# RWKV-7 scan of an encoder layer: heads stacked on partitions, an inverse and its transpose kept in PSUM, three chunks in one TensorE order

## The reference

```python
def step(S, inp):                       # S: (B, H, 64, 64), f32
    r_t, w_t, k_t, v_t, kk_t, a_t = inp
    sa = jnp.einsum('bhij,bhj->bhi', S, -kk_t)
    S = (S * w_t[:, :, None, :] + sa[..., None] * (kk_t * a_t)[:, :, None, :]
         + v_t[..., None] * k_t[:, :, None, :])
    y = jnp.einsum('bhij,bhj->bhi', S, r_t)
    return S, y
_, y = lax.scan(step, zeros, xs, reverse=reverse)   # y of both directions is added
```

## Time and profile before

| What | Value |
|---|---|
| median of 2 runs | 4515.17 us (4513.25 to 4517.09) |
| profiled execution, its own time | 4511.47 us |
| span of its trace | 4509.7 us |
| mean granted TensorE clock | 0.944 of full |
| instructions | 73891 |
| TensorE busy | 86% of the span, 30776 matmuls |
| DVE / ScalarE / GpSimd busy | 49% / 24% / 11% |
| mean DMA rate | 54 GB/s |

### The profile page before, as it was taken

One profiled execution on the slowest core, in us unless ns is written; L12 is line 12 of the kernel. 1 busy time (PEld: TensorE's weight loads), 2 busy tenths in 40 slices (PEclk: granted clock), 3 DMA queues, 4 the chain that ended last, 5 costly groups with the idle time before them and its releaser, 6 DMA issues. The chain is left out here.

```text
span 4509.7 us, 73891 instructions
## 1 busy us (share of the span) xinstructions
PE 3898.8 (86%) x30776; PEld 3260.3 (72%) x30776; DVE 2232.0 (49%) x2980; ACT 1070.0 (24%) x1635; POOL 500.4 (11%) x407
## 2 busy tenths in 40 slices
PE   7999999988997355588888886888788899999997
PEld 6888888866885342477777764676677788888886
DVE  4445444462002757777777754242224444444445
ACT  2111111122112455333333333222222111111112
POOL 0000000010000420243344321010001000000000
PEclk9999999998998677899999997998899999999999
DMA  2111011002222026311111122300110101101101
GB/s 100 41 42 39 30 42 42 19 10 108 84 84 114 1 84 190 112 52 35 52 52 52 35 83 70 121 14 29 38 33 19 52 28 42 42 30 40 42 19 47
DMA packets 70916, 244.32 MB, mean 54 GB/s; under 512 B 5056, under 2 KB 30912, under 8 KB 64320
## 3 DMA queue, kind: packets, MB, share of 16 engines
q1 hardware_dynamic: 64528, 219.56, 14.2%
q10 hardware_dynamic: 6192, 21.89, 1.2%
HBM read 185.38 MB, written 56.05 MB: 54 GB/s over the span
## 5 line engine op out<-in xcount | busy, mean ns | idle before, releaser
L292 DVE TENSOR_TENSOR main_acc<-main_acc,ffn_psum 128x512 f32<-128x512 f32 (+1 forms) x1056 | 617.3, 598 | 855.1 <-PE ffn_psum L215 854.4
L204 PE MATMUL ffn_psum<-x_xh,ffn_wi_h 128*128 128x512 f32 (+1 forms) x2112 | 525.0, 357 | 52.5 <-DVE ffn_wi_l L281 52.5
L204 PE MATMUL ffn_psum<-x_xl,ffn_wi_h 128*128 128x512 f32 (+1 forms) x2112 | 525.2, 357 | 0.0
L204 PE MATMUL ffn_psum<-x_xh,ffn_wi_l 128*128 128x512 f32 (+1 forms) x2112 | 525.2, 357 | 0.0
L204 PEld LDWEIGHTS ffn_psum<-x_xh,ffn_wi_h 128*128 128x128 f32 x2112 | 372.5, 188 | 120.2 <-DVE ffn_wi_l L281 52.9
L204 PEld LDWEIGHTS ffn_psum<-x_xh,ffn_wi_l 128*128 128x128 f32 x2112 | 350.1, 189 | 60.3
L204 PEld LDWEIGHTS ffn_psum<-x_xl,ffn_wi_h 128*128 128x128 f32 x2112 | 349.6, 188 | 60.9
L215 PE MATMUL ffn_psum<-ffn_hid_h,ffn_wo_h 128*128 128x512 f32 (+1 forms) x1056 | 381.3, 361 | 12.9 <-DVE ffn_hid_l L300 10.0
L215 PE MATMUL ffn_psum<-ffn_hid_h,ffn_wo_l 128*128 128x512 f32 (+1 forms) x1056 | 378.1, 358 | 0.0
L215 PE MATMUL ffn_psum<-ffn_hid_l,ffn_wo_h 128*128 128x512 f32 (+1 forms) x1056 | 377.4, 357 | 0.0
L256 ACT CAST ffn_hid_h<-ffn_hid 128x1280 fp32r<-128x1280 f32 x44 | 55.7, 1265 | 1090.4 <-DVE ffn_hid L298 1090.4
(11 more groups left out here) (315 smaller groups left out, 6756.3 us busy)
## 6 DMA issues: line engine op xcount, KB each, us to landing
ffn_w_raw_in<-ffn_w_in_dram SPq DMA_DIRECT2D x44, 1024.0 KB, 6.8
rws_pack<-pack SPq DMA_DIRECT2D x40, 900.0 KB, 4.6
ffn_w_raw_out<-ffn_w_out_dram SPq DMA_DIRECT2D x44, 512.0 KB, 3.6
proj<-mixin_stage ACTq DMA_DIRECT2D x27, 640.0 KB, 3.0
mixin_w_raw<-mix_w_in_dram SPq DMA_DIRECT2D x27, 512.0 KB, 3.5
pack<-rwp_pack SPq DMA_DIRECT2D x4, 2580.0 KB, 10.7
rwp_raw<-proj SPq DMA_DIRECT2D x15, 640.0 KB, 8.5
kv_w_raw<-ca_w_kv_dram SPq DMA_DIRECT2D x16, 512.0 KB, 3.5
```

Of the source, the lines that this page charges most:

```text
L204: mm = nc.tensor.matmul(ps[:, at + c * BANK:at + c * BANK + tn], w[:, slot, cols], x[:, k, t0:t0 + tn], start=(k == 0 and j == 0), stop=(k ...
L292: nc.vector.tensor_tensor(acc[:, o, t0:t0 + tn], acc[:, o, t0:t0 + tn], ps[:, at:at + tn], ALU.add).then_inc(added, 1)
```

## The change

The phase is written anew for the same mathematics. Head 0 of each pair stays on lanes 0 to 63 and head 1 on lanes 64 to 127 throughout, with no padding: every tile is 128 x (2 directions x 4 pairs x 64), and one product works on 64 lanes of one half of the array (`own`) or crosses from one half's lanes to the other half's outputs (`other`). The whole-array transposes go. Where the transpose of X was needed, a second matrix Z, the transpose, is built beside X: both stay in PSUM over all levels, and a level adds to them by accumulating products (`extend`); ScalarE copies each of them out after every level. Transposed rows of b and k are made by products with a 64x64 identity (`turn_rows`); v is transposed once, in the preparation, and loaded by its own DMA. Each instruction of DVE, ScalarE and GpSimd covers both directions where it covered one. The decay edge of a chunk is folded into one factor (`carry`), so h takes one product a chunk. GpSimd makes the scaled b, k, a and r and the first level; DVE keeps the masks, h and the addition to the output. In a step n three chunks are in work: the state of n, levels 1 to 5 of the inverse of m = n + 1, and the products of p = n + 2; the step list runs from n = -2. Buffers hold two to four chunks. In the masks, `before_pair` and `upto` give way to `within` and `first` of the same widths.

All that concerns a group of products has this form; `state_u`, `state_out`, `with_rows`, `turn_rows` and `first_x` are built like those shown, with 16, 48, 32 (128 columns wide), 32 and 16 products.

```diff
-R_COL, V_COL, G_COL = 0, C, 2 * C
+V_COL, R_COL, G_COL = 0, C, 2 * C
...
+        V_GROUPS = tuple((g, min(8, N_CHUNKS - g), (6 + n % 2) * BANK) for n, g in enumerate(range(0, N_CHUNKS, 8)))
...
+                pe.wait_ge(next_added, 6 * (t + 2))
+                for n, (c0, cn, at) in enumerate(V_GROUPS):
+                    if n == 2 or t:
+                        pe.wait_ge(v_set, 3 * t + max(n - 1, 0))
+                    for c in range(cn):
+                        for h in range(2):
+                            lanes = slice(h * C, (h + 1) * C)
+                            mm = nc.tensor.matmul(ps[lanes, at + c * C:at + (c + 1) * C], vr[lanes, (c0 + c) * C:(c0 + c + 1) * C],
+                                                  stack_ident[lanes], start=True, stop=True)
+                    mm.then_inc(v_turned, 1)
...
-                nc.scalar.copy(part(V_COL), view(vr[:])).then_inc(copied, 1)
+                for n, (c0, cn, at) in enumerate(V_GROUPS):
+                    act.wait_ge(v_turned, 3 * t + n + 1)
+                    nc.scalar.copy(pack[:, c0:c0 + cn, V_COL:V_COL + C], ps[:, at:at + cn * C].rearrange("p (c t) -> p c t", t=C)).then_inc(v_set, 1)
...
+        BOTH, PAIR, EDGED = [P, 2, 4, C], [P, 2, 4, 2, C], [P, 2, 4, C + 1]
+        pack, v = slots("pack", [P, 2, 4, PACK - R_COL], 2), slots("v", BOTH, 4)
+        x, z, y, inverse = m_.sb("x", BOTH), m_.sb("z", BOTH), m_.sb("y", BOTH), m_.sb("inverse", BOTH)
+        AT_X, AT_Z, AT_Y, AT_U, AT_H, AT_O = range(6)
+        AT_GB, AT_GK, AT_ROWS = (6, 7), (5, 6), (7, 4)
...
+            for c in range(N_CHUNKS):
+                if c >= 2:
+                    sp.wait_ge(exps, 2 * (c - 1))
+                    sp.wait_ge(bk_set, 2 * (c - 1))
+                    sp.wait_ge(ar_set, 2 * (c - 1))
+                if c >= 4:
+                    sp.wait_ge(o_done, c - 3)
                 for d in DIRS:
+                    sp.dma_start(pack[c % 2][:, d], pack_d[chunk_of(c)[d]][:, :, R_COL:PACK]).then_inc(loaded[c % 2], 16)
+                    sp.dma_start(v[c % 4][:, d], pack_d[chunk_of(c)[d]][:, :, V_COL:V_COL + C]).then_inc(loaded[c % 2], 16)
...
+            def scale(c):
+                pool.wait_ge(loaded[c % 2], 64 * (c // 2 + 1))
+                pool.wait_ge(exps, 2 * (c + 1))
+                if c >= 2:
+                    pool.wait_ge(b_turned, c - 1)
+                    pool.wait_ge(k_turned, c - 1)
+                nc.gpsimd.tensor_tensor(bk[c % 2][:, :, :, 0], packed(c, B_COL), now(grown[c % 2]), ALU.mult).then_inc(bk_set, 1)
+                nc.gpsimd.tensor_tensor(bk[c % 2][:, :, :, 1], packed(c, K_COL), now(grown[c % 2]), ALU.mult).then_inc(bk_set, 1)
+                if c >= 3:
+                    pool.wait_ge(o_done, c - 2)
+                nc.gpsimd.tensor_tensor(ar[c % 3][:, :, :, 0], packed(c, KK_COL), before(decayed), ALU.mult).then_inc(ar_set, 1)
+                nc.gpsimd.tensor_tensor(ar[c % 3][:, :, :, 1], packed(c, R_COL), now(decayed), ALU.mult).then_inc(ar_set, 1)
+                if c >= 1:
+                    if c >= 4:
+                        pool.wait_ge(h_set, c - 2)
+                    nc.gpsimd.tensor_tensor(carry[(c - 1) % 3][:], edge(grown[(c - 1) % 2]), edge(grown[c % 2]), ALU.mult).then_inc(carried, 1)
+            def first_level(c):
+                pool.wait_ge(masked_b, 2 * (c + 1))
+                nc.gpsimd.tensor_tensor(first[:], gb[c % 2][:, :, :, 0], first_mask, ALU.mult).then_inc(first_set, 1)
+                pool.wait_ge(first_set, c + 1)
+                if c:
+                    pool.wait_ge(z_done, ZS * (c - 1) + 1)
+                nc.gpsimd.tensor_tensor(w0[:], first[:], all_ident, ALU.add).then_inc(w0_set, 1)
+            def step(n, m, p):
+                if p is not None:
+                    scale(p)
+                    first_level(p)
...
+            def first_z(c):
+                pe.wait_ge(w0_set, c + 1)
+                if c:
+                    pe.wait_ge(inverse_set, c)
+                for n, (d, q) in enumerate(TILES):
+                    for e in range(2):
+                        mm = product(bank(AT_Z)[other(e), col(d, q)], stack_ident[own(e)], w0[own(e), d, q], start=(n == 0), stop=False)
+                mm.then_inc(z_done, 1)
+            def lower(c, level):
+                pe.wait_ge(x_set, XS * c + level)
+                if level > 1 or c:
+                    pe.wait_ge(y_set, XS * c + level - 1)
+                for d, q in TILES:
+                    for e in range(2):
+                        mm = product(bank(AT_Y)[other(e), col(d, q)], gb[c % 2][own(e), d, q, 0], x[own(e), d, q])
+                mm.then_inc(y_done, 1)
+            def extend(c, level):
+                pe.wait_ge(y_set, XS * c + level)
+                pe.wait_ge(z_set, XS * c + level)
+                for d, q in TILES:
+                    if level < LEVELS - 1:
+                        for e in range(2):
+                            mx = product(bank(AT_X)[own(e), col(d, q)], z[other(e), d, q], y[other(e), d, q], start=False)
+                    for e in range(2):
+                        mz = product(bank(AT_Z)[other(e), col(d, q)], y[other(e), d, q], z[other(e), d, q], start=False)
+                if level < LEVELS - 1:
+                    mx.then_inc(x_done, 1)
+                mz.then_inc(z_done, 1)
+            def state_rhs(n):
+                pe.wait_ge(h_set, n + 1)
+                pe.wait_ge(masked_k, 2 * (n + 1))
+                if n:
+                    pe.wait_ge(u_set, n)
+                o = bank(AT_U)
+                for d, q in TILES:
+                    for e in range(2):
+                        product(o[other(e), col(d, q)], gk[n % 2][own(e), d, q, 0], v[n % 4][own(e), d, q], stop=False)
+                    for e in range(2):
+                        mm = product(o[other(e), col(d, q)], ar[n % 3][own(e), d, q, 0], h[n % 2][own(e), d, q], start=False)
+                mm.then_inc(rhs_done, 1)
...
+            def state_h(n):
+                pe.wait_ge(u_set, n + 1)
+                pe.wait_ge(b_rows_set, n + 1)
+                pe.wait_ge(k_rows_set, min(n + 2, N_CHUNKS))
+                o = bank(AT_H)
+                for d, q in TILES:
+                    for e in range(2):
+                        product(o[own(e), col(d, q)], k_rows[n % 2][own(e), d, q], v[n % 4][own(e), d, q], stop=False)
+                    for e in range(2):
+                        mm = product(o[own(e), col(d, q)], b_rows[n % 2][own(e), d, q], u[own(e), d, q], start=False)
+                mm.then_inc(h_done, 1)
...
+            def step(n, m, p):
+                if n >= 0:
+                    state_rhs(n)
+                if m is not None:
+                    first_z(m)
+                    lower(m, 1)
+                if n >= 0:
+                    state_u(n)
+                if m is not None:
+                    extend(m, 1)
+                if n >= 0:
+                    state_h(n)
+                if m is not None:
+                    lower(m, 2)
+                if n >= 0:
+                    state_out(n)
+                if m is not None:
+                    extend(m, 2)
+                if p is not None:
+                    with_rows(p, 0, AT_GB, with_b)
+                if m is not None:
+                    lower(m, 3)
+                if p is not None:
+                    with_rows(p, 1, AT_GK, with_k)
+                if m is not None:
+                    extend(m, 3)
+                if p is not None:
+                    turn_rows(p, 0)
+                if m is not None:
+                    lower(m, 4)
+                if p is not None:
+                    turn_rows(p, 1)
+                if m is not None:
+                    extend(m, 4)
+                    lower(m, 5)
+                if p is not None:
+                    first_x(p)
+                if m is not None:
+                    extend(m, 5)
...
+            def take_x(c, level):
+                act.wait_ge(x_done, XS * c + level + 1)
+                if level or c:
+                    act.wait_ge(y_done, XS * c + level)
+                nc.scalar.copy(x[:], as_both(bank(AT_X))).then_inc(x_set, 1)
+            def take_z(c, level):
+                act.wait_ge(z_done, ZS * c + level + 1)
+                nc.scalar.copy(z[:], as_both(bank(AT_Z))).then_inc(z_set, 1)
...
+            def step(n, m, p):
+                if p is not None:
+                    exponentials(p)
+                if n >= 0:
+                    take_rhs(n)
+                if m is not None:
+                    take_z(m, 0)
+                if n >= 0:
+                    take_u(n)
+                if m is not None:
+                    for level in (1, 2, 3):
+                        take_x(m, level)
+                        take_z(m, level)
+                if p is not None:
+                    take_rows(p, 0)
+                    take_rows(p, 1)
+                if m is not None:
+                    take_x(m, 4)
```

(80 more changed lines are left out.)

427 lines of the change are left out of this document (154 added, 273 removed).

## The result

The changed kernel takes 4270.34 us (median of 2 runs, 4267.43 to 4273.25) against 4515.17, a ratio of 0.9458 with a 95% interval of 0.9417 to 0.9498. The forecast was 4088 us, 4045 to 4180: the sign was right, the gain is 245 us in place of 427, and the time lies outside the range. The profiled execution took 4267.43 us. Measured times are medians over the executions of a kernel; of the version with one product of 512 columns one execution took 15958.97 us, the others 4263 to 4268, and it is left out.

The account below looks back on a forecast made before the run. The level chain (lower, mask, extend, x copy) was to bound the new step at 18.9 us: prologue 38, eighteen steps 340, then 17.5 and 6.6, together 402 us for 829.5; 427 us saved gave 4088 us, range 4045 to 4180.

Parts of the forecast that it names:

- Sixteen occupy TensorE for 0.47 us: New step's groups: 16 products of 64 columns were priced at 0.47 us of TensorE, 29 ns each.
- 12.1 + 1.8 = 14 us: TensorE's issue in a new step: 416 products of 64 columns and 32 of 128, 14 us in all.
- the count of 304: Products of 64 columns in an old step by the diff's lists, part of 21 us of issue in 40.9 us.
- the chain of 18.9 us: New step: lower, mask, extend, copy of x, 3.29 us a level, giving 18.9 us a step in place of 40.9.
- Later loads cost nothing: Scan: loads issued about 8 us into a step, read some 30 us later, so they add no time.
- The rivals of the clock: Steady scan steps: clock falls to 1.2 GHz, products cost about 1.7 times, step near 28 us, total 4260; chance 0.08.
- of GpSimd: Scan steps: GpSimd's scale products come too late for the b products; total 4110 to 4175 us, chance 0.17.
- chains that add up: Scan steps: fillers' waits stop TensorE, inverse, state and preparation add to 30 us a step, total 4300; chance 0.05.
- Products across the halves: Rival, slower than before: such products don't overlap, 190 ns more each, 39.5 us a step, total 4880; chance 0.04.
- the rule of the one bank: Skill page's rule that row tiles cannot write one PSUM bank at once; judged contradicted by present pairs starting every 29 ns.
- no collision: Scan step: the h product on DVE was forecast to collide with GpSimd and take 1.71 us, bounds 0.7 and 2.1.
- The start: Scan's beginning: first loads taken at 6 us, bounds 4.8 and 12.2, within a prologue of 38 us.

## Why the prediction was wrong

- **The failed step** is the unit price "Sixteen occupy TensorE for 0.47 us", and with it "12.1 + 1.8 = 14 us". It took matmul records for products: the 16 records in the earlier trace rows are 8 products, and the count of 304 was never set against the records of a step. With the earlier trace rows, 14880 matmul records in 20 steps are 744 a step, twice 304 + 32 plus 72. Measured: 0.94 us for 16 products, and 110 ns, not 55, for one of 128 columns. At these prices the old step was 304 x 58 ns + 32 x 110 ns + 72 x 145 ns = 31.6 us of TensorE's 40.9, not 21, and the new one is (416 - 128) x 58 ns + 4 x 1.0 + 3.5 = 24.2 us: by this estimate TensorE, not the chain of 18.9 us, would have set the forecast step, at 24 to 25 us with instructions in time.
- **The bound that was missing** is the supply of instructions. No rival named it, and the unit price hid it: at 14 us a step the array would have asked for a block each 2 us. The stops are 52.3 us in 17.8 steps, 2.9 us each; with 24.2 us of array and 0.6 of waits for the x copies they make 27.7 of the 28.1 us. The tests of it are the runs with more records and without loads; that 1792 records are 7.06 blocks of 254, and 4.03 us for each give 28.4 us, only restates the count of packets. Before, the same queue brought 108 packets in 750 us of the scan (1900 to 2650 us), 6.9 us apart, so nothing in that time showed it as a limit:

```profile
q8 instruction: 108, 1.77, 1.0%
```

- **"Later loads cost nothing"** was right of their landing and wrong of their cost: 32 us without them, as the packets then come every 3.79 us.
- **What held:** masks 0.69 us, copies 0.59, the exponentials 0.64, a clock near 1.00 in the steps, loads landing in time, and no loss in the preparation (the scan starts at 1845.3, before at 1846.1). The rivals of the clock, of GpSimd and of chains that add up are out by that clock and by the 0.6 us a step for which TensorE waits for another engine. One figure of the clock's rival is off: 1.97 / 1.09 is 1.8, not 1.7.
- **Products across the halves** follow each other at 58 ns, as those within the halves do. That rival, the slower one, is out. The 29 ns by which the prediction judged the rule of the one bank were records, half a product each; what speaks for a pair running side by side in one bank is the run with two products of 512 columns, one for each half: 0.86 us for both, and 1.06 us for the single product of 512 columns.
- **GpSimd** needs 1.19 us for the operands with a pitch of 65, not 1.40, and ends before the h product, which takes 0.69 us, not 1.71: no collision.

```profile
L1316 POOL TENSOR_TENSOR rws_ar<-rws_pack,rws_decayed x20: 1170/1187/1206, 1858.5 to 2379.3; 128x512 f32<-128x512 f32 x20
```

  The two meet in the run with one tile of eight. The h product that starts at 2102.79 us, 0.40 us before the end of GpSimd's instruction, takes 0.94 us, 0.25 more than alone; the one at 1982.28, 0.71 us before such an end, takes 1.26, 0.57 more. GpSimd's next instruction, begun meanwhile, takes 1.65 in place of 1.19. By the Trainium skill's page "SBUF — State Buffer", section "Who interferes with whom", the ports that the two share are an exclusive lock. The trace agrees: h waited for the rest of the instruction under way, less 0.14 us both times. By this the 1.71 us of the earlier trace rows would depend on where the two meet; no run tests that.
- **The start**: 8.5 us from the first load to the exponentials in place of 6, within the bounds; the rest of the 10 us would fit chunk 0's products at twice the price, with a clock of 0.81, which no run tests.

Open: why a block takes at least some 3.3 us with no load about, so how far 26.4 us a step without loads is supply and how far array (24.2 us by the corrected sum). Nor is the pace a fixed one: in the three runs with fewer records and loads as in the change, 120 or 121 packets came in the 500 us in place of 124. So 32 products left out gave 1.2 us a step and not the 2.0 of half a block, and first_z in few products gave 0.3 us or less; why the packets came later there isn't shown.

## What to carry to other kernels

Before a price is taken from a row, count the program's products against the records in the trace; an f32 product of 64x64 weights has two matmul records and two weight loads here, a 128x128 transpose one. Where many small products replace few large ones, weigh the count of instructions too: 254 records in some 3.8 us, away from loads, were about the pace of this scan, whatever the order on the array. Then loads that seem hidden compete with the instructions, and here spreading them over the step took 18 us off.

## What the runs showed that was not expected

- Products of 64x64x64 in f32 follow each other at 58 ns where a group uses two quarters of the array, and at 31 ns where four take turns; yet issuing extend over 1.7 us in place of 1.0 changed nothing in a step whose instructions are late.
- A load of 1.8 MB delays the instruction packets: stops up to 3.2 us with it, 0.9 without. The Trainium skill's page "Trainium Architecture — The Big Picture", section "The software stack", has the instruction streams moved into each engine at load time; the trace shows more of them coming during the run, 124 packets within 500 us.
- In the run with one tile of eight TensorE was busy for 90.6 of 150 us, in short groups between waits, and the granted clock was 0.50, the level of 1.2 GHz; the step of 15.3 us is at that level.
